# The first mixer's instruction order: from one step of every chain per round to steps chosen by running time estimates

## What is computed

```python
h = _rmsnorm(x, norm_mix_pre[l]).astype(dt)
z = h @ w_in[l]
z_a, z_b, z_c, z_d = _split(z, GROUP_SPLITS)
y_a = _rwkv7(z_a, ...)     # state recurrence over 512 steps, 4 heads of 64
y_b = _mlstm(z_b, ...)     # gated linear attention, 4 heads
y_c = _swa(z_c, ...)       # attention in a window of 128, 4 heads
y_d = _fox(z_d, ...)       # causal attention with forget gates, 4 heads
y = jnp.concatenate([y_a, y_b, y_c, y_d], axis=-1).astype(dt)
x = x + _rmsnorm(y @ w_out[l], norm_mix_post[l]).astype(dt)
```

## Time and profile before

| | |
|---|---|
| median of 3 runs | 1794.56 us (1794.3 to 1795.21) |
| the profiled execution's own time | 1789.02 us |
| its span, first to last instruction | 1787.0 us |
| mean granted TensorE clock | 0.970 |
| first mixer up to the output projection | some 371 us of the span |
| one projection piece, start to start, in 44 to 55 us | 2.72 us |

### The profile page before, as it was taken

The page is one execution under the profiler, slowest core; times in us unless marked ns, Lnnn a source line. Parts: engine busy times, 40 slices in busy tenths (PEclk is TensorE's granted clock), DMA queues, the critical chain, the costliest instruction groups (busy, mean ns, idle before and its releaser), DMA issues.

```text
span 1787.0 us, 21171 instructions
## 1 busy us (share of the span) xinstructions
PE 1674.1 (94%) x8578; PEld 1349.9 (76%) x8578; DVE 856.9 (48%) x1425; ACT 680.6 (38%) x1214; POOL 248.9 (14%) x211
## 2 busy tenths in 40 slices
PE   5799799877999999998999999999999999999995
PEld 3577576565788888876888888877887788888884
DVE  4566464545555553226444443357455444444332
ACT  4434445344543333235333323334353433333222
POOL 0000000002222220004222210010010022222001
PEclk9999999888999999998999999999999999999998
DMA  4111111031233223331322233322122232222331
GB/s 157 49 60 48 47 36 37 1 106 48 84 112 99 95 94 98 97 99 38 118 95 94 95 101 97 97 90 83 48 83 88 78 106 94 95 94 92 99 100 63
DMA packets 44129, 148.21 MB, mean 83 GB/s; under 512 B 5064, under 2 KB 6144, under 8 KB 44032
## 3 DMA queue, kind: packets, MB, share of 16 engines
q1 hardware_dynamic: 40032, 140.53, 24.6%
q10 hardware_dynamic: 4000, 6.33, 1.0%
HBM read 144.73 MB, written 2.10 MB: 82 GB/s over the span
## 4 chain that ended last, share of the span: by engine, by line
PE 89%; DVE 6%; ACT 4%; issue 1%; POOL 0%; DMA 0%; DVEq 0%; ACTq 0%
PE bank L142 77%; PE bank L268 6%; PE bank L236 3%; DVE t L119 2%; DVE t L127 2%; ACT t L110 2%; PE bank L146 2%; ACT L110 1%; DVE t L197 0%; ACT t L195 0%; POOL t L119 0%; DVE t L124 0%; ACT t L115 0%; DVE t L136 0%; DMA t<-in_cst 0%
## 5 line engine op out<-in xcount | busy, mean ns | idle before, releaser
L142 PE MATMUL bank<-t 128*128 128x512 f32 (+7 forms) x7578 | 1529.3, 361 | 48.9 <-DVE t L119 20.9
L142 PEld LDWEIGHTS bank<-t 128*128 128x128 f32 (+3 forms) x7578 | 1166.5, 180 | 326.1 <-issue 45.1
L197 DVE TENSOR_TENSOR t<-t 128x512 fp32r<-128x512 f32 (+1 forms) x540 | 403.4, 778 | 466.2 <-ACT t L195 465.8
L195 ACT ACTIVATE t<-t 128x512 fp32r<-128x512 f32 (+1 forms) x540 | 311.5, 613 | 267.5 <-PE bank L268 221.8
L119 POOL TENSOR_TENSOR t<-t 128x512 f32<-128x512 f32 (+1 forms) x179 | 236.9, 1324 | 1225.4 <-DVE t L119 586.8
L110 ACT ACTIVATE t<-t 128x512 f32<-128x512 f32 (+5 forms) x308 | 180.6, 605 | 373.4 <-DVE t L119 175.4
L119 DVE TENSOR_TENSOR t<-bank,t 128x512 f32<-128x512 f32 (+3 forms) x246 | 148.1, 615 | 239.3 <-PE bank L268 216.1
L268 PE MATMUL bank<-t 128*128 128x512 f32 x516 | 200.9, 389 | 0.0
L115 ACT ACTIVATE t<-t 128x512 fp32r<-128x512 f32 (+3 forms) x89 | 53.7, 617 | 253.2 <-POOL t L119 246.7
L119 DVE TENSOR_TENSOR t<-t 128x512 f32<-128x512 f32 (+9 forms) x168 | 99.9, 612 | 64.7 <-ACT t L110 62.8
L236 PE MATMUL bank<-t 128*128 128x512 f32 x288 | 82.1, 452 | 37.5 <-DVE t L127 32.5
(11 more groups left out here) (21 smaller groups left out, 113.6 us busy)
## 6 DMA issues: line engine op xcount, KB each, us to landing
t<-in_ffn_w_up SPq DMA_DIRECT2D x88, 512.0 KB, 3.9
t<-in_w_in SPq DMA_DIRECT2D x50, 512.0 KB, 3.3
t<-in_ffn_w_down SPq DMA_DIRECT2D x48, 512.0 KB, 3.5
t<-in_ffn_w_gate SPq DMA_DIRECT2D x44, 512.0 KB, 3.3
t<-in_ffn_w_down SPq DMA_DIRECT2D x24, 384.0 KB, 3.1
t<-in_w_out SPq DMA_DIRECT2D x16, 512.0 KB, 3.4
t<-in_xt SPq DMA_DIRECT2D x8, 256.0 KB, 5.4
t<-in_xt ACTq DMA_DIRECT2D x8, 256.0 KB, 5.3
```

The costliest lines, as they stand in the source:

```text
L142: fn = lambda e: e.matmul(out, w, x, start=start, stop=stop, skip_group_check=True)
L195: self.p.av.put(lambda e: e.activation(hi, raw, ACT.Copy), self.s_head, 1, (self.s_load[u % RAW], 16 * (u // RAW + 1)), (self.s_used, i - ...
L197: self.p.dv.put(lambda e: e.tensor_tensor(lo, raw, hi.bitcast(F), SUB), self.s_tail, 1, (self.s_head, i + 1))
```

## The change

Every queue keeps an estimate `at` of the time at which it gets to its end: each operation adds a cost worked out from its shape, each wait lifts `at` to the estimated time of the token. An estimate of each token is kept in `due`: the queue's time plus 0.2 us (PE) or 0.1 us, or plus 6 us for a DMA. Chains now yield the tokens that their next step waits for. `drive_by` takes the first chain in the list whose tokens are due by PE's estimate; if there is none it issues the next piece of the projection; once there are no pieces it takes the chain that is due first. `attention` and `mlstm` stand first in the list. The work of all chains, their tiles and banks stay. The second mixer goes on with `drive`.

```diff
 class Queue:
-    def __init__(self, nc, ctx, name):
+    def __init__(self, nc, ctx, name, due):
...
+        self.due, self.at, self.lag = due, 0.0, 0.2 if name == "pe" else 0.1
     def wait(self, *points):
...
                 self.items.append((None, d[0], d[1]))
+                self.at = max(self.at, self.due.get((id(d[0]), d[1]), 0.0))
...
-    def put(self, fn, sem, by, *points):
+    def put(self, fn, sem, by, *points, us=0.1):
         self.wait(*points)
         self.items.append((fn, sem, by))
+        self.at += us
+        if sem is not None:
+            n = self.due[id(sem)] = self.due.get(id(sem), 0) + by
+            self.due[id(sem), n] = self.at + (self.lag if by == 1 else 6.0)
...
+def ready(points, due):
+    if isinstance(points, list):
+        return max([ready(d, due) for d in points], default=0.0)
+    return 0.0 if points is None else due.get((id(points[0]), points[1]), 0.0)
...
 class Prog:
+    def cost(self, out, q, two=False):
+        if q is self.po:
+            return 0.2 + 0.0022 * width(out)
+        if q is self.av:
+            return 0.15 + 0.0009 * width(out)
+        return 0.15 + (0.0012 if two else 0.001) * width(out)
     def act(self, out, in_, func, *deps, bias=0.0, scale=1.0, accum=None):
+        us = self.cost(out, self.av)
+        if func not in (ACT.Copy, ACT.Square, ACT.Identity):
+            table = ACT.Exp if func == ACT.Ln else func
+            us += 0.0 if table == self.table else 1.3
+            self.table = table
...
     def mm(self, out, w, x, start, stop, *deps, last=False):
+        us = width(x) / 2400 + 0.013
+        if w.dtype != R:
+            us = (max(width(x), width(w)) / 1200 + 0.015) * (0.5 if w.shape[0] <= 64 else 1) * (
+                0.5 if width(w) <= 64 else 1)
...
 def pipeline(groups):
     groups, live = list(groups), []
     while groups or live:
         if groups:
-            live += groups.pop(0)
-        for g in list(live):
+            live += [[g, None] for g in groups.pop(0)]
+        yield [t for _, t in live]
+        for one in list(live):
             try:
-                next(g)
+                one[1] = next(one[0])
             except StopIteration:
-                live.remove(g)
-        yield
+                live.remove(one)
...
+def drive_by(p, chains, filler):
+    live, filling = [[g, None] for g in chains], True
+    def step(one):
+        try:
+            one[1] = next(one[0])
+        except StopIteration:
+            live.remove(one)
+    while live or filling:
+        for one in [c for c in live if c[1] is None]:
+            step(one)
+        open_ = [(ready(c[1], p.due), n, c) for n, c in enumerate(live) if c[1] is not None]
+        now = [c for t, n, c in open_ if t <= p.pe.at]
+        if now:
+            step(now[0])
+        elif filling:
+            filling = next(filler, "end") != "end"
+        elif open_:
+            step(min(open_, key=lambda c: c[:2])[2])
...
         def attention():
-            for _ in range(3):
-                yield
+            yield [t]
             b = ab.next()
             m = p.mm(b.t[0:4, 0:384], oh[0:32, 768:772], oh[0:32, 0:384], True, True, t, b.free, last=True)
...
         def rwkv(j):
             rt, kt, vt = (tok["rkv", j, n] for n in range(3))
+            yield [vt, tok["w"]]
...
             y = p.act(t1[:, :], kk[:, :], ACT.Square, x)
-            yield
+            yield [y, ta]
...
-        chains = [rwkv(0), rwkv(1), masks(0), masks(1)]
-        rest = [finish(j, g2) for j in range(2) for g2 in range(2)] + [conv(0), conv(1), splits(), first_out()]
-        drive([proj()] + chains + rest + [attention(), mlstm()])
+        chains = [rwkv(0), rwkv(1), masks(0), masks(1)] + [finish(j, g2) for j in range(2) for g2 in range(2)]
+        chains = [attention(), mlstm(), conv(0), conv(1)] + chains + [splits(), first_out()]
+        drive_by(p, chains, proj())
```

More of the change, by code:

```diff
@@ L94, in __init__ @@
         self.nc, self.ctx = nc, ctx
-        self.pe = Queue(nc, ctx, "pe")
-        self.av = Queue(nc, ctx, "act")
-        self.dv = Queue(nc, ctx, "dve")
-        self.po = Queue(nc, ctx, "pool")
+        self.due = {}
+        self.pe, self.av, self.dv, self.po = (Queue(nc, ctx, n, self.due) for n in ("pe", "act", "dve", "pool"))
+        self.table = None
         self.count = 0
@@ L110, in act @@
         return self.av.do(lambda e: e.activation(out, in_, func, bias=bias, scale=scale,
-                                                 **({} if accum is None else {"accum_out": accum})), *deps)
+                                                 **({} if accum is None else {"accum_out": accum})), *deps, us=us)
     def copy(self, out, in_, *deps, q=None):
-        if q is None or q is self.av:
-            return self.av.do(lambda e: e.activation(out, in_, ACT.Copy), *deps)
-        return q.do(lambda e: e.tensor_copy(out, in_), *deps)
+        q = q or self.av
@@ L118, in tt @@
+        us = self.cost(out, q)
+        if q is self.av:
+            return q.do(lambda e: e.activation(out, in_, ACT.Copy), *deps, us=us)
+        return q.do(lambda e: e.tensor_copy(out, in_), *deps, us=us)
     def tt(self, out, a, b, op, *deps, q=None):
-        return (q or self.dv).do(lambda e: e.tensor_tensor(out, a, b, op), *deps)
+        q = q or self.dv
+        return q.do(lambda e: e.tensor_tensor(out, a, b, op), *deps, us=self.cost(out, q, True))
     def ts(self, out, a, s1, s2, op0, op1, *deps, q=None):
+        q = q or self.dv
@@ L122, in ts @@
+        us = self.cost(out, q)
         if s2 is None:
-            return (q or self.dv).do(lambda e: e.tensor_scalar(out, a, s1, None, op0), *deps)
-        return (q or self.dv).do(lambda e: e.tensor_scalar(out, a, s1, s2, op0, op1), *deps)
+            return q.do(lambda e: e.tensor_scalar(out, a, s1, None, op0), *deps, us=us)
+        return q.do(lambda e: e.tensor_scalar(out, a, s1, s2, op0, op1), *deps, us=us)
     def stt(self, out, a, s, b, op0, op1, *deps):
-        return self.dv.do(lambda e: e.scalar_tensor_tensor(out=out, in0=a, scalar=s, in1=b, op0=op0, op1=op1), *deps)
+        return self.dv.do(lambda e: e.scalar_tensor_tensor(out=out, in0=a, scalar=s, in1=b, op0=op0, op1=op1), *deps,
+                          us=self.cost(out, self.dv, True))
@@ L138, in mset @@
     def mset(self, out, v, *deps, q=None):
-        return (q or self.po).do(lambda e: e.memset(out, v), *deps)
+        q = q or self.po
+        return q.do(lambda e: e.memset(out, v), *deps, us=self.cost(out, self.dv))
     def mm(self, out, w, x, start, stop, *deps, last=False):
         fn = lambda e: e.matmul(out, w, x, start=start, stop=stop, skip_group_check=True)
-        return self.pe.do(fn, *deps) if last else self.pe.quiet(fn, *deps)
+        us = width(x) / 2400 + 0.013
+        if w.dtype != R:
+            us = (max(width(x), width(w)) / 1200 + 0.015) * (0.5 if w.shape[0] <= 64 else 1) * (
+                0.5 if width(w) <= 64 else 1)
@@ L145, in tr @@
+        return self.pe.do(fn, *deps, us=us) if last else self.pe.quiet(fn, *deps, us=us)
     def tr(self, out, in_, ident, *deps, last=False):
         fn = lambda e: e.transpose(out, in_, ident)
-        return self.pe.do(fn, *deps) if last else self.pe.quiet(fn, *deps)
+        return self.pe.do(fn, *deps, us=0.12) if last else self.pe.quiet(fn, *deps, us=0.12)
 RAW, CUT = 2, 6
@@ L238, in pair_steps @@
                     if n >= 3 - signal:
-                        pe.put(fn, self.s_used, 1, xl(k)[1])
+                        pe.put(fn, self.s_used, 1, xl(k)[1], us=0.227)
                     else:
-                        pe.quiet(fn, xl(k)[1])
-            yield
+                        pe.quiet(fn, xl(k)[1], us=0.227)
         self.at += 4
@@ L652, in attention @@
                 yield
+            yield [tok["gates"]]
             X, G2 = hb[:, 0:T], hb[:, T:2 * T]
@@ L737, in mlstm @@
                 yield
+            yield [tok["mv", 1], tok["mk"], tok["mq"]] + used["fox"]
             free0, mb = used["fox"], ab
@@ L780, in product @@
             def product(h):
-                yield
-                yield
-                yield
+                yield None
+                yield None
+                yield list(pt)
                 b = mb.next()
```

104 lines of the change are left out of this document (56 added, 48 removed).

## The result

| | before | after |
|---|---|---|
| median of 6 executions, us | 1794.43 (1788.85 to 1795.4) | 1782.11 (1777.98 to 1786.73) |
| ratio to before | | 0.9936 [0.9913, 0.9958] |
| profiled execution, us | 1789.02 | 1779.48 |
| its span, us | 1787.0 | 1777.5 |
| mean granted clock | 0.97 | 0.97 |

The changed kernel was measured twice more, on other chips: 0.9952 [0.9933, 0.9971] and 0.9951 [0.9934, 0.9967]. The sign held, and the time lies in the range for 8 in 10 (1744 to 1792) but outside the forecast's own range (1749 to 1780); the size did not hold. Instead of 30 us some 9 to 12 were gained (0.0048 to 0.0064 of 1794), and rival 2 (the stall moves to the tail, 1782) named both the time and the place. Most executions of the kernel before lie near 1786 or near 1795 us, in shares that differ from chip to chip, so medians are compared through the ratio and its interval.

A forecast was written before the change was run, and what follows sets the result against it. Bound: the order of PE's queue in the first mixer's early stretches, the mLSTM chain in its last. Gains 28.9 + 8 + 8 = 45, less 5 + 6 + 4 = 15, give 30 us: 1764 us, own range 1749 to 1780, 8 in 10 1744 to 1792.

The forecast's parts named there:

- rival 2: First mixer: pieces are spent early, fox and mLSTM then run bare, mLSTM's 74 us don't shrink; 1782 us, chance 0.20.
- What bounds the kernel: First mixer: PE's in-order queue holds pieces behind waiting matmuls in early stretches; the mLSTM chain bounds the last one.
- Early stalls: 27 to 95 and 213 to 240 us: pieces fill all PE idle time, 28.9 us gained, lower bound 17.7.
- Clock in those stretches: The same early stretches: clocks of 0.90, 0.90 and 0.75 recover, 8 us gained, bounds 5 and 13.6.
- Tail: mLSTM's heads at the mixer's end: stepped ahead of RWKV whenever due, 8 us gained, between none and 15.
- (a): Pieces run out earlier, so fox and the second RWKV pair partly lack filler: 5 us lost, between nothing and 15.
- (b): Planner counts Ln and Exp as one table, so steps are released too soon: 6 us lost, at most 18.
- (c): Chains share four PSUM banks whose release is in no token, so steps wait for copies: 4 us lost, at most 15.
- (d): The 512 KB read of bias rows may take up to 8.5 us against 6 planned: 0 to 2.5, taken as 0.
- POOL: POOL has 7.91 us of work in the mixer's 344 us; being passed by pieces costs it nothing.
- Rival 3: RWKV's 60 steps released too soon, PE waiting with pieces behind: about 20 us slower, 1815 us, chance 0.12.

The follow-up runs named there:

- k1: Changed kernel without RWKV's second pair of heads (steps, masks and finish left out): 1723.37 us, one execution.
- e2: Changed kernel with the planner's prices for fp32 matmuls and for Ln and Exp tables set to the trace's: 1783.1 us, 0.9934 of before.
- e10: e8 with three pieces right behind the second RWKV pair's first product with bones, and two instead of three before its second: 1780.57 us, 0.9948 of before.
- k2: Changed kernel without mLSTM's work after fox: 1753.19 us, one execution.
- e3: Changed kernel with steps released 2.7 us early, and POOL waiting for its own last instruction at the start of mLSTM's steps: 1824.93 us, 1.019 of before.
- e8: Kernel before, with eight rounds instead of three for rel_bias and seven pieces put by hand ahead of RWKV products that waited: 1774.9 us, 0.9926 of before.
- e12: e11 with the two pieces before the second product with bones also moved behind the chain's own operations: 1770.14 us, 0.9872; again 1773.81 us, 0.9906.
- e11: e10 with its three pieces moved to the end of that step, behind its DVE and ACT operations: 1777.66 us, 0.9909 of before.

## Why the prediction came out at over twice the gain

- **What bounds the kernel: right.** The gaps of 27 to 95 and 213 to 240 us were RWKV's own latency with pieces standing behind it, and the pieces went into them.
- **Early stalls, 28.9 us: right in size.** 24.0 us of idle time went before the last piece. The rel_bias wait and the 5.86 us went completely. The 3.40 us at 83.94 was counted as gone and stays, as 3.90 at 98.06. So does the second pair's 9.22 us: it is there as 11.22 us at 266.41, among what the tail lost.
- **Clock in those stretches, 8 us: right there, lost elsewhere.** The clock rose to 1.00 in the three stretches, and fell from 1.00 to 0.82 in 240 to 297 us. Busy time for the same matmuls fell by 1.4 us in all, not 8.
- **Tail, 8 us gained: this step failed, with (a).** The prediction let mLSTM speed up because it is stepped first, and took the early end of the pieces as 5 us. Instead, idle time behind the last piece grew by 16.5 us (19.0 to 35.5), where term (a) had its bound at 15, and the heads' reads went from 38.7 to 58.7 us. What it had not counted: the pieces saved up to 300 us had been the cover of fox and of the second pair's first steps. The first pair took 191 us instead of 144, since twelve more pieces (33 us) and more of attention's steps (15 us) went between its steps. So the second began 45 us later, went bare at its own 89 to 90 us, and ended where it always had. The 43 us that mLSTM was ahead went into waiting beside it, as k1 shows: 28.0 us between the reads without it.
- **(b) Estimates too short, 6 us given back: no such loss.** Before the pieces end the Ln–Exp group costs PE 0.90 us, at 73.37, and not in RWKV: a piece waits there for its bank, since ACT's cut for the next piece stood behind the two loads and DVE waited 3.87 us for it. Right prices (e2) gave nothing. The two loads remain: in e10 the Ln and the Exp at 217.68 and 219.62 us each have one of 1.28 us before them, as in the earlier trace rows. The Trainium skill (ScalarE: Activation LUTs, Table sets: the hidden batching unit) has one load for Ln followed by Exp; no run here shows that.
- **(c) Shared banks, 4 us: about right.** Waits on ACT copies are 7.1 us in ten against 2.8 in seven before. The 3.90 us at 98.06 is a wait for a bank too, but for one of RWKV's own.
- **(d) and POOL: right at nothing.** The read of bias rows was issued at 120.01 and no wait on it appears.
- **Rivals.** Rival 2 was the case, by its mechanism and its time. Its argument against itself, that the second pair has 30 steps to put into the gaps, was the wrong one: k2 shows that these steps make gaps rather than fill them. Rival 3 exists but not in the change, which releases steps late rather than early; e3 shows its price.

The prediction's own tests said as much: no PE idle over 2 us before some 250 us failed once (3.90 at 98.06), the stretch of 240 to 297 us, which had next to no idle time, now has 15.9, the output projection was to start at about 341 and started at 361.7, and the tail was to be under 56 us from the first spread to the last read. The reads alone now take 58.7.

## What to carry to other kernels

Filler that goes into one wait is taken from a later one: before pricing a filled gap as won, look at what runs when the filler is gone, and whether the serial chains that end the stage start or go any sooner. Work that looks like one engine's takes a place in every in-order queue that it touches, so filler is better issued behind the waiting chain's own operations on the other engines than in front of them (8.18 us of wait against 1.68 at one place, with nothing moved on PE; the same move at the other place showed no gain in the trace). A planner that releases a step only when the queue's end passes the step's due time hardly idles the engine while it has filler (7.1 us here) and stretches the chain: by 47 us over 30 steps.

## What the runs showed of the hardware

- The same matmuls of this mixer are busy for 289 to 322 us, in kernels that spread the idle time differently: 288.8 in e8, 292.1 in e12, 292.5 after the change, 322.0 in e3, whose waits lie among all steps. The clock of a stretch went from 1.00 to 0.82 when 15.9 of its 57 us became idle.
- The same idle time does not always cost the same clock: 30 records at 324.72 in e11 take 8.53 us, the same 30 at 330.14 in e10 take 4.85, both behind 2.10 us of idle time. The granted clock is 0.50 in the one and 1.00 in the other.
- ACT goes on within 0.01 to 0.02 us of a table load's 1.28 us; in e10 three loads with the five operations around them fill 216.16 to 222.55, and PE's wait of 8.18 us ends behind them (8.30 in e8).
